# A two-layer hybrid trunk on one core: latent up-projection in full groups, selection steps inside the latent attention, and four changes of order

## The reference

```python
# B: latent attention, 4 heads, 64 unrotated and 32 rotated columns, values 64
q = (rms_norm(c_q, q_norm_g) @ w_uq).reshape(b, s, 4, 96)
q = concatenate([q[..., :64], apply_rotary(q[..., 64:], *rope)])
kv = (rms_norm(c_kv, kv_norm_g) @ w_ukv).reshape(b, s, 4, 128)
k_nope, v = kv[..., :64], kv[..., 64:]
k_rope = apply_rotary(k_rope, *rope)            # one for all heads
o = causal_block_attention(q, concatenate([k_nope, k_rope]), v, 96 ** -0.5)
# D: sparse attention: an indexer scores all keys, 128 keys are kept per query
score = einsum('bqhs,bqh->bqs', relu(logits), iwb)
_, sel = top_k(score, 128)
o = attention over the kept keys
# after each branch
x = x + (g_a * y_a + g_b * y_b + g_c * y_c + g_d * y_d) @ w_o
```

## Time and profile before

| | |
|---|---|
| median of 3 runs | 2044.9 us (2044.44 to 2045.82) |
| profiled execution, its own time | 2043.76 us |
| its span, first to last instruction | 2041.9 us |
| mean granted TensorE clock | 0.996 |
| TensorE busy | 1987.6 us (97%) |
| VectorE busy | 1087.1 us (53%) |
| ScalarE busy | 768.7 us (38%) |
| Pool busy | 737.3 us (36%) |

### The profile page before, as it was taken

One profiled execution on the slowest core, in us unless ns is written; L12 is line 12 of the kernel. 1 busy time (PEld: TensorE's weight loads), 2 busy tenths in 40 slices (PEclk: granted clock), 3 DMA queues, 4 the chain that ended last, 5 costly groups with the idle time before them and its releaser, 6 DMA issues.

```text
span 2041.9 us, 31745 instructions
## 1 busy us (share of the span) xinstructions
PE 1987.6 (97%) x13120; PEld 1526.7 (75%) x13120; DVE 1087.1 (53%) x1807; ACT 768.7 (38%) x1206; POOL 737.3 (36%) x553
## 2 busy tenths in 40 slices
PE   6999999999999999999999999999999999999997
PEld 5788787756667888888867877776566778888886
DVE  8785555896833422222487756379876343222223
ACT  5442523344353442322354353234344433332323
POOL 3431313422324444444444132243213344444442
PEclk9999999999999999999999999999999999999999
DMA  6220112211312332333332111123122223233332
GB/s 231 75 81 28 57 34 78 84 59 50 122 55 77 114 102 93 95 101 93 97 121 90 47 37 58 43 79 95 52 78 81 68 85 101 93 101 95 94 102 73
DMA packets 51647, 169.42 MB, mean 83 GB/s; under 512 B 5728, under 2 KB 14048, under 8 KB 50864
## 3 DMA queue, kind: packets, MB, share of 16 engines
q1 hardware_dynamic: 50448, 163.11, 24.9%
q0 software_dynamic: 1056, 4.28, 0.6%
HBM read 160.29 MB, written 7.08 MB: 82 GB/s over the span
## 4 chain that ended last, share of the span: by engine, by line
PE 84%; DVE 11%; ACT 3%; issue 1%; DMA 0%; POOL 0%; ACTq 0%; SPq 0%; DVEq 0%
PE bank_a L491 13%; PE bank_a L497 13%; PE bank_a L492 13%; PE bank_v L497 7%; PE bank_v L491 7%; PE bank_v L492 7%; PE bank_v L567 4%; PE bank_v L645 3%; DVE arena L1518 1%; PE bank_a L804 1%; PE bank_f L599 1%; PE bank_f L605 1%; PE bank_f L578 1%; DVE mg L1524 1%; PE bank_a L793 1%
## 5 line engine op out<-in xcount | busy, mean ns | idle before, releaser
L451 POOL TENSOR_TENSOR w_lo<-ring,w_hi 128x512 fp32r<-128x512 f32 x536 | 729.6, 1382 | 1207.4 <-ACT w_hi L1184 1207.2
L491 PE MATMUL bank_a<-h_hi,w_hi 128*128 128x512 f32 x1296 | 523.8, 404 | 3.9 <-DVE h_lo L1557 3.9
L492 PE MATMUL bank_a<-h_lo,w_hi 128*128 128x512 f32 x1296 | 505.7, 390 | 0.0
L1184 ACT ACTIVATE w_hi<-ring 128x1024 fp32r<-128x1024 f32 x268 | 281.5, 1050 | 222.6 <-DVE arena L2118 212.4
L497 PE MATMUL bank_a<-h_hi,w_lo 128*128 128x512 f32 x1296 | 321.4, 390 | 0.0
L491 PEld LDWEIGHTS bank_a<-h_hi,w_hi 128*128 128x128 f32 x1296 | 243.4, 188 | 75.0 <-issue 19.4
L492 PEld LDWEIGHTS bank_a<-h_lo,w_hi 128*128 128x128 f32 x1296 | 243.6, 188 | 57.1 <-issue 8.1
L497 PEld LDWEIGHTS bank_a<-h_hi,w_lo 128*128 128x128 f32 x1296 | 244.0, 188 | 50.8
L491 PE MATMUL bank_v<-parts,w_hi 128*128 128x512 f32 x640 | 251.3, 393 | 1.4 <-DVE parts L2087 1.4
L492 PE MATMUL bank_v<-parts,w_hi 128*128 128x512 f32 x640 | 249.1, 389 | 0.0
L1518 DVE TENSOR_TENSOR sg<-bank_v,sg 128x512 f32<-128x512 f32 x112 | 77.4, 691 | 310.5 <-PE bank_v L497 239.3
(11 more groups left out here) (296 smaller groups left out, 2505.5 us busy)
## 6 DMA issues: line engine op xcount, KB each, us to landing
ring<-in_w SPq DMA_DIRECT2D x268, 512.0 KB, 3.5
out_ring<-in_w SPq DMA_DIRECT2D x64, 128.0 KB, 3.4
x_dram<-arena SPq DMA_DIRECT2D x2, 2048.0 KB, 8.8
arena<-x_dram SPq DMA_DIRECT2D x2, 2048.0 KB, 9.1
arena<-in_x SPq DMA_DIRECT2D x2, 1024.0 KB, 9.4
out_x<-arena SPq DMA_DIRECT2D x4, 512.0 KB, 3.7
consts<-in_const SPq DMA_DIRECT2D x1, 1189.0 KB, 13.6
arena<-tabs POOLq DMA_DIRECT2D x2, 512.0 KB, 3.9
```

The costliest lines, as they stand in the source:

```text
L451: ins = nc.gpsimd.tensor_tensor(w_lo[:, g % SPLIT, ks, :], raw, w_hi[:, g % SPLIT, ks, :].bitcast(F32), ALU.subtract)
L491: mm(b[:], w_hi[:, s, k, :], hi[:, k, :], start=k == 0, stop=False)
L492: mm(b[:], w_hi[:, s, k, :], lo[:, k, :], start=False, stop=False)
L1184: act_fn(w_hi[:, g % SPLIT, :, :], ring[:, g % RING, :, :], ACT.Copy).then_inc(S["split_hi"], 1)
```

## The change

1. **Full groups.** The columns of the up-projection weights are reordered on the host: the queries' 64 unrotated columns of the four heads, then their 32 rotated ones; the keys of all heads, then the values of all heads. TensorE makes the queries in three full groups, the third being all rotated parts in one tile `qr`, and the keys in two. ScalarE copies each head's half of a bank to partitions 0 to 63 (two copies a bank). One rotation product serves all heads. VectorE multiplies the whole tile twice and adds four times, 32 partitions each, writing to partitions 64 to 95 of each head. The rotary table is loaded four times, once for each head's partitions.
2. **Selection.** VectorE does 3 steps ahead of the latent attention, not 9, and 8 inside it, behind steps 5, 7, 9, 11 and 13.
3. **First scores.** In both attentions the first pair of scores is made ahead of one (latent) or both (sparse) output products of the merge before; VectorE merges these tiles behind its second score operation.
4. **ScalarE** copies a finished gate before the attention output, and splits the next weights after both.
5. **Pool** waits with the low part of each layer's fifth unit for all 8 low parts of the activations. The six table stores go to SP, behind its sixth load.

```diff
+SPARE = {5: 1, 7: 2, 9: 1, 11: 2, 13: 2}
...
@@ SP
+                if g == 5:
+                    sp.wait_ge(S["tab"], 1)
+                    for i, nm in enumerate(("cos", "sin")):
+                        for rows in (quarter(0), quarter(1)):
+                            sp.dma_start(tabs[0, i, rows], POS[nm][quarter(0), :]).then_inc(tab_out, 16)
+                        sp.dma_start(tabs[1, i, quarter(1)], POS[nm][quarter(1), :]).then_inc(tab_out, 16)
@@ Pool
                 pool.wait_ge(S["split_hi"], g + 1)
+                if u == RAW_UNITS + 1:
+                    pool.wait_ge(S["n_h"], at(l, "n_h", 2 * KT))
...
-                if g == 3:
-                    pool.wait_ge(S["tab"], 1)
...
-                    pool.dma_start(Mv["tab"][quarter(1), :, :], ...).then_inc(tab_m_here, 16)
+                    for h in range(H):
+                        pool.dma_start(Mv["tab"][32 * h:32 * h + 32, :, :], ...).then_inc(tab_m_here, 16)
@@ TensorE
+                    if i == 0:
+                        behind_scores()
...
-                for h in range(H):
+                for i in range(3):
                     b, reader, emptied = banks.next("a", "m_q")
                     for k in range(2):
-                        ins = mm(b[0:96, :], pr("uq")[:, k * 384 + h * 96:k * 384 + (h + 1) * 96], Mv["cq"][:, k, :], ...)
+                        ins = mm(b[:], pr("uq")[:, k * 384 + i * P:k * 384 + (i + 1) * P], Mv["cq"][:, k, :], ...)
-                for h in range(H):
-                    mm(b[0:64, :], pr("ukv")[:, h * P:h * P + C], misc[:, 0, :], start=True, stop=True).then_inc(a_full, 1)
+                for f in range(2):
+                    mm(b[:], pr("ukv")[:, f * P:(f + 1) * P], misc[:, 0, :], start=True, stop=True).then_inc(a_full, 1)
...
-                for h in range(H):
-                    pe.wait_ge(S["m_q"], at(l, "m_q", h + 1))
-                    mm(b[0:96, :], cst("rot_m")[0:96, 0:96], Mv["q"][0:96, h, :], start=True, stop=True).then_inc(v_full, 1)
-                merge(l, 0, 1, 3)
+                pe.wait_ge(S["m_q"], at(l, "m_q", 3))
+                mm(b[:], cst("rot_q"), Mv["qr"], start=True, stop=True).then_inc(v_full, 1)
+                last = gates(l, 0, 3)
+                merge_outputs(1, last[:1])
...
+                          lambda: merge_outputs(1, last[1:]))     # latent attention
+                          lambda: merge_outputs(0, last))         # sparse attention
@@ ScalarE
+                    fill(i)
                     if i >= 4 and i % 2 == 0:
                         ...
-                    fill(i)
+                    if gate_done(i):
+                        split_next()
@@ VectorE
-                go_on(9)
+                go_on(3)
...
-                    tt(Mv["tmp"][rp, :], b[rp, :], sin, MUL)        # for each head
-                    tt(x_, x_, cos, MUL)
-                    v.tensor_tensor(x_, x_, Mv["tmp"][rp, :], ADD)
+                tt(Mv["tmp"], b[:], Mv["tab"][:, 1, :], MUL)       # once
+                tt(Mv["qr"], Mv["qr"], Mv["tab"][:, 0, :], MUL)
+                    v.tensor_tensor(Mv["q"][rp, h, :], Mv["qr"][rows, :], Mv["tmp"][rows, :], ADD)   # for each head
-                merge(l)
-                attention(l, "m", ...)
+                merge(l, tiles=1)
+                attention(l, "m", ..., lambda i: merge(l, tiles=1) if i == 1 else go_on(SPARE.get(i, 0)))
```

More of the change, by code:

```diff
@@ L1041, in _ @@
                 attention(l, "m", lambda h, qt: Mv["q"][0:96, h, qt * P:(qt + 1) * P],
-                          lambda h, n: Mv["k"][0:96, h, 0:n], lambda i: next(pieces) if i in GATE_STEPS else None)
+                          lambda h, n: Mv["k"][0:96, h, 0:n], lambda i: next(pieces) if i in GATE_STEPS else None,
+                          lambda: merge_outputs(1, last[1:]))
                 numbers.append(gate(l, 1, 3))
@@ L1045, in _ @@
                 merge_outputs(0, numbers)
-                for i in range(2, 4):
-                    merge(l, 1, 0, i)
+                merge(l, 1, 0, 2)
+                last = gates(l, 1, 3)
                 pe.wait_ge(S["d_rot"], at(l, "d_rot", 8))
@@ L1052, in _ @@
                 attention(l, "d", lambda h, qt: Dv["q"][quarter(h % 2), h // 2, qt * P:(qt + 1) * P],
-                          lambda h, n: Dv["k"][quarter(h % 2), h // 2, 0:n], lambda i: next(pieces) if i in GATE_STEPS else None)
+                          lambda h, n: Dv["k"][quarter(h % 2), h // 2, 0:n], lambda i: next(pieces) if i in GATE_STEPS else None,
+                          lambda: merge_outputs(0, last))
                 numbers.append(gate(l, 3, 3))
@@ L1430, in _ @@
                 indexed_sig()
[L1431 removed]
+                for f in range(2):
                     act.wait_ge(a_full, filled.next())
                     b = filled.bank()
[L1434 removed]
+                    for p_ in range(2):
+                        ins = act_fn(Mv["q"][0:C, 2 * f + p_, :], b[quarter(p_), :], ACT.Copy)
+                    ins.then_inc(S["m_q"], 1)
+                act.wait_ge(a_full, filled.next())
+                b = filled.bank()
+                act_fn(Mv["qr"], b[:], ACT.Copy).then_inc(S["m_q"], 1)
                 act.wait_ge(S["d_acc"], at(l, "d_acc", 24))
[L1436 removed]
+                for f in range(2):
                     act.wait_ge(a_full, filled.next())
                     b = filled.bank()
[L1439 removed]
+                    for p_ in range(2):
+                        ins = act_fn(Mv["k"][0:C, 2 * f + p_, :], b[quarter(p_), :], ACT.Copy)
+                    ins.then_inc(S["m_k"], 1)
                 for half in range(2):
@@ L1678, in _, with merge @@
             merged = [0]
-            def merge(l, first=False):
-                for _ in range(2):
+            def merge(l, first=False, tiles=2):
+                for _ in range(tiles):
                     n = merged[0]
@@ L2061, in _ @@
                     dve.wait_ge(S["m_kr"], reached("m_kr"))
+                dve.wait_ge(v_full, filled.next())
+                b = filled.bank()
+                tt(Mv["tmp"], b[:], Mv["tab"][:, 1, :], MUL)
+                tt(Mv["qr"], Mv["qr"], Mv["tab"][:, 0, :], MUL)
                 for h in range(H):
-                    dve.wait_ge(v_full, filled.next())
-                    b = filled.bank()
-                    tt(Mv["tmp"][rp, :], b[rp, :], sin, MUL)
-                    x_ = Mv["q"][rp, h, :]
-                    tt(x_, x_, cos, MUL)
-                    v.tensor_tensor(x_, x_, Mv["tmp"][rp, :], ADD).then_inc(S["m_rot"], 1)
-                    dve.wait_ge(S["m_rot"], reached("m_rot"))
-                merge(l)
-                attention(l, "m", Mv, 96 ** -0.5, lambda qt: Mv["bias"][:, (3 - qt) * P:T])
+                    rows = slice(32 * h, 32 * h + 32)
+                    ins = v.tensor_tensor(Mv["q"][rp, h, :], Mv["qr"][rows, :], Mv["tmp"][rows, :], ADD)
+                ins.then_inc(S["m_rot"], 1)
+                dve.wait_ge(S["m_rot"], reached("m_rot"))
+                merge(l, tiles=1)
+                attention(l, "m", Mv, 96 ** -0.5, lambda qt: Mv["bias"][:, (3 - qt) * P:T], lambda i: merge(l, tiles=1) if i == 1 else go_on(SPARE.get(i, 0)))
                 go_on(9)
@@ L2078, in _ @@
                     pass
-                merge(l)
-                attention(l, "d", Dv, C ** -0.5, lambda qt: Dv["bias"][:, qt, 0:(qt + 1) * P] if qt else cst("causal"))
+                attention(l, "d", Dv, C ** -0.5, lambda qt: Dv["bias"][:, qt, 0:(qt + 1) * P] if qt else cst("causal"), lambda i: merge(l) if i == 1 else None)
                 for i in range(5):
```

48 lines of the change are left out of this document (22 added, 26 removed).

## The result

The changed kernel takes 2020.55 us (median; 2020.27 to 2020.67) against 2044.67 us (2042.67 to 2045.82) for the kernel before: a ratio of 0.9887, with a 95% interval of 0.9875 to 0.9899. It is 24.1 us faster; 26.2 were forecast. The profiled execution took 2020.27 us, its span is 2018.4 us against 2041.9, and the mean granted clock is 0.997 against 0.996.

What follows compares the result with a forecast made beforehand. TensorE was taken as the bound, busy 1987.6 of 2041.9 us. The terms 12.4 + 4.5 + 4.0 + 6.1 - 0.8 = 26.2 us, taken from 2044.9, gave 2018.7 us, range 2014.8 to 2025.0.

Steps and rivals of the forecast that it cites:

- signs of being right: 12, 4 and 2 records; no waits at attention starts or line 599; low parts at most 1.8 us; first group 5.5 us.
- signs of being wrong: TensorE waiting for normalisation mid latent attention, VectorE's gaps gone there, or a new wait at the low-rank products.
- Full groups: Up-projection and rotation: 14 records fewer a layer at 0.43 us, plus short waits; 12.4 us saved, ends 12.0 and 12.7.
- First scores: Attention starts: scores ahead of merge products remove TensorE's waits for normalisation and bank; 4.5 us saved, ends 3.5 and 5.1.
- ScalarE's order: Gates in pieces: copying the finished gate first removes TensorE's bank wait at line 599; 4.0 us saved, ends 3.0 and 4.3.
- Pool's fifth weights: Layer starts: Pool's subtraction behind the low parts stops delaying VectorE; 6.1 us saved, ends 4.0 and 6.3.
- Slots: Latent attention: eight selection steps in five slots, mostly in VectorE's idle gaps; 0.8 us charged, ends 0 and 5.2.
- second rival: Latent attention: slots 7 and 13 too small, Pool stretching VectorE; 5.2 us for the 0.8 charged, 2023.1 us; chance 0.14.
- Tables: Table stores moved to the sync queue, latent table in four loads: costed at 0, ends -0.3 and +0.5 us.
- The first: Port collision moves to VectorE's shift mixes, TensorE waits at low-rank products: 2024.8 us, more likely 2021.7; chance 0.08.
- The third: Latent attention: slots not covered at all, stands followed by lower clock; 38 us lost against 26.2 saved, 2056; chance 0.03.
- The fourth: Full groups cost more than their records, or VectorE's partition-moving operations are slow; 12.4 us lost, 2031; chance 0.03.

Runs made afterwards that it cites:

- the kernel without slots: Changed kernel with nine selection steps ahead of the latent attention and none inside: 2031.17 us, ratio 0.994 to the kernel before.
- the first experiment: Changed kernel with the up-projection, its copies and the rotation done one head at a time again: 2032.1 us, ratio 0.9945 to the kernel before.

## Why the prediction held, point by point

Of its signs of being right all came but one: TensorE still waits at the attentions' starts (0.77 and 1.29 us). Of its signs of being wrong two came, both small: a wait for VectorE's normalisation inside the latent attention (0.73 us, near its end), and no gap left on VectorE behind slots 7 and 13.

**Full groups: 12.4 forecast, 12.8 in the trace (2 x 6.39).** The 14 records at 0.43 us and the short waits held; 12.8 is 0.1 above the upper end. One product has the same price with 64, 96 or 128 columns of its stationary operand.

**First scores: 4.5 forecast, 1.0 measured. This is the mis-sized term**, outside its range of 3.5 to 5.1. The prediction had TensorE's times right within its own frame: the gates 10.7 us behind the up-projection (10.27 measured to their first record), the first scores 23.4 us behind it (461.6 - 438.2; measured 457.38 - 434.06 = 23.3), VectorE idle ahead of them (5.12 us). It also named the culprit, that "VectorE's one or two merge tiles now lie between the first and the second normalisation", and put it at "a few tenths". A tile is 1.4 us, two are 2.8, and the normalisation came 0.77 and 1.29 us late for them, so TensorE's order had only about 0.6 (latent) and 1.5 (sparse) to spare. Following VectorE's order as it had followed TensorE's, operation by operation to the second normalisation, would have shown it. In the sparse attention ScalarE's exponential is late as well, behind a load of its function table, so the merges don't start there until 539.6:

```profile
537.05 1.28 ACT L1238 ACT_TABLE_LOAD   x1
...
538.87 0.16 DVE L1741 RECIPROCAL att<-att 128x1 f32<-128x1 f32 x1 [2.35 <-ACT arena L1238]
```

**ScalarE's order: 4.0 forecast, 4.3 gone, 3.1 when taken back alone.** The step holds. What it lacked is that a stand of TensorE's is also VectorE's time.

**Pool's fifth weights: 6.1 forecast, 6.2 in the trace, 5.7 to 6.0 by taking it back.** Pool's subtraction now begins at 42.18, right behind the last low part. Some 1.5 of the 6.2 us are the clock that the profiled execution of before had lost. The forecast took that execution for the rule; in two others the same collision cost 4.4 and 4.8 us.

**Slots: 0.8 charged, 1.5 measured.** The second rival (slots 7 and 13 too small with a stretch by Pool) fits slot 13 and was wrong for slot 7: there Pool's subtraction starts at 471.42, but the steps are maxima and replacements and keep their 0.56 and 0.54 us beside it. Its price of 2.6 us a layer was 0.73. It explains half a microsecond or so of the miss in the sum, not a case of its own.

**Tables: 0 forecast**, +0.1 when put back, no different from nothing.

**The rivals.** The first fell: there is no stretch of the mixes that TensorE would wait for; its wait at the low-rank products is 0.8 us in both layers together, where it was 0.7. Pool's late subtraction (42.18 to 44.72) met operations that read a bank, the three of L1586 in 0.69 us each, as long as such an operation takes alone. Its next one, from 46.31 to 49.50, did stretch two of the mixes, to 1.66 and 1.67 us from 0.69 and 0.75, and TensorE's list of waits shows nothing of it. The Trainium skill's page "SBUF — State Buffer", section "Who interferes with whom", says that a VectorE instruction with at most one input in SBUF doesn't contend with GpSimd unless it is in one of the two-port modes, and that one with two such inputs contends with a GpSimd instruction that reads SBUF. Both rows agree; that TensorE would wait didn't follow. The third, a lower clock behind many stands, didn't occur in the changed kernel, but the kernel without slots shows its mechanism: one stand of 4.39 us and 2.35 us lost to the clock behind it. The fourth fell with the first experiment.

**The sum.** 26.2 against 24.1: the first scores gave 3.5 less and the slots 0.7 less, the groups, ScalarE and Pool 0.4, 0.3 and 0.1 more, and 0.7 of the span stay unassigned; the medians differ by 0.6 more than the two spans. The terms' errors partly cancel (4.2 us too much in two of them, 0.8 too little in three, and 1.3 in none), so part of the closeness of the total is luck, and it doesn't vouch for each term.

## What to carry to other kernels

- Where two engines take turns, walk through both queues up to the operation that the first will wait for next. The order in which TensorE was moved ahead took 1.0 us off the waits; moving one merge tile of VectorE's, two operations, by one slot in each attention took off 4.1.
- Before work is moved on VectorE, lay it against Pool's timeline. Pool's subtractions stand at the same places whatever VectorE does, and an operation that reads two operands from SBUF beside one took up to five times as long here (3.3 us for 0.68).
- Take parts back one at a time in the final kernel: 4.3 us of ScalarE's wait were worth 3.1, since another engine had lived in that time.

## What was unexpected of the hardware

- A stand of 2.26 us was followed by a granted clock of 0.63 in one profiled execution, and one of 2.24 us at the same place by 1.00 in another. The first cost 1.46 us on top of the stand, the second nothing. In a stand of 4.39 us the clock fell before the stand ended and cost 2.35 us on top. At this place a stand near 2 us had two prices.
- Pool's subtraction is two instructions (x2 in its rows). One low part beside it took 3.29 us in one placing, where Pool's pair took 2.51; in another two took up to 1.78 us each and Pool's pair 3.35. The pair started at 40.77 in the first and at 40.60 in the second. That the start relative to VectorE's operation decides is a guess; no run moved it alone.
- Not only additions of two operands suffer: a multiplication and addition of scalars on 128x384 (L2021), with one tensor operand, took 1.33 us beside Pool, for 0.36.
